# A decoder block's input projection: the last 40 tiles as 2 x 2 blocks with seven half-depth products

## The reference

```python
h = rms_norm(x, norm_g)
proj = h @ w_in            # 1024 -> 8704 columns
u_ssm, z_ssm, q, k, v, z_attn, q_mem, z_mem, gate_logits = split(proj)
y = gelu(s5_ssm(u_ssm)); y = y * sigmoid(y @ w_glu + b_glu); o_ssm = y * silu(z_ssm)
o_attn = dilated_window_attention(q, k, v)  # 3 groups of 4 heads, dilation 1, 4, 16
o_attn = (o_attn weighed by softmax of the groups' log sums) * silu(z_attn)
o_mem = cross_attention(q_mem, rms_norm(mem) @ w_mem_kv) * silu(z_mem)
gates = sigmoid(gate_logits + b_gate)
merged = sum over branches of gates * (o_branch @ w_branch)
out = rms_norm(x + merged @ w_out)
```

## Time and profile before

| | before |
|---|---|
| median of three runs | 2456.7 us |
| span of the profiled execution | 2455.0 us |
| TensorE busy | 2438.3 us (99%), 12622 matmuls |
| DVE busy | 1397.7 us (57%) |
| ACT busy | 588.0 us (24%) |
| GpSimd busy | 190.4 us (8%) |
| mean granted TensorE clock | 0.999 |

### The profile page before, as it was taken

One profiled execution on the slowest core, in us unless ns is written; L12 is line 12 of the kernel. 1 busy time (PEld: TensorE's weight loads), 2 busy tenths in 40 slices (PEclk: granted clock), 3 DMA queues, 4 the chain that ended last, 5 costly groups with the idle time before them and its releaser, 6 DMA issues.

```text
span 2455.0 us, 31834 instructions
## 1 busy us (share of the span) xinstructions
PE 2438.3 (99%) x12622; PEld 1981.9 (81%) x12622; DVE 1397.7 (57%) x2636; ACT 588.0 (24%) x1275; POOL 190.4 (8%) x328
## 2 busy tenths in 40 slices
PE   9999999999999999999999999999999999999998
PEld 8888888888877777787777788888888888888887
DVE  7356776767734444413544443444345778787785
ACT  5222222222211111113333343333251111110201
POOL 0000000000011111110000000011100000000000
PEclk9999999999999999999999999999999999999999
DMA  8232433343454444442332343477654865857571
GB/s 327 99 93 76 106 114 117 107 120 95 115 151 137 149 160 142 151 156 73 105 134 95 121 147 122 161 228 243 205 206 164 285 182 168 248 177 242 159 233 59
DMA packets 171033, 378.67 MB, mean 154 GB/s; under 512 B 27008, under 2 KB 72164, under 8 KB 163717
## 3 DMA queue, kind: packets, MB, share of 16 engines
q1 hardware_dynamic: 134980, 235.03, 31.0%
q0 software_dynamic: 34864, 139.51, 16.9%
q10 hardware_dynamic: 1040, 2.10, 0.2%
HBM read 245.10 MB, written 131.43 MB: 153 GB/s over the span
## 4 chain that ended last, share of the span: by engine, by line
PE 97%; DVE 1%; ACT 1%; issue 0%; DMA 0%; DVEq 0%; SPq 0%; ACTq 0%
PE bank L137 29%; PE bank L139 29%; PE bank L138 28%; PE bank L2285 2%; PE bank L2328 1%; PE bank L2306 1%; PE bank L2194 1%; PE bank L2197 1%; PE bank L2264 1%; PE bank L2180 1%; PE bank L2242 1%; PE bank L2316 1%; ACT tsc L1188 1%; PE bank L2145 0%; PE bank L2247 0%
## 5 line engine op out<-in xcount | busy, mean ns | idle before, releaser
L137 PE MATMUL bank<-h_hi,w_hi 128*128 128x512 f32 (+1 forms) x2720 | 1083.7, 398 | 1.4 <-DVE h_lo L1434 1.4
L139 PE MATMUL bank<-h_hi,w_lo 128*128 128x512 f32 (+1 forms) x2720 | 1057.4, 389 | 0.0
L138 PE MATMUL bank<-h_lo,w_hi 128*128 128x512 f32 (+1 forms) x2720 | 1056.3, 388 | 0.0
L137 PEld LDWEIGHTS bank<-h_hi,w_hi 128*128 128x128 f32 x2720 | 510.8, 188 | 117.2 <-issue 13.6
L139 PEld LDWEIGHTS bank<-h_hi,w_lo 128*128 128x128 f32 x2720 | 510.7, 188 | 108.1
L138 PEld LDWEIGHTS bank<-h_lo,w_hi 128*128 128x128 f32 x2720 | 511.3, 188 | 103.0 <-issue 1.7
L129 DVE CAST w_hi<-w_raw 128x1024 fp32r<-128x1024 f32 (+1 forms) x121 | 83.3, 688 | 310.1 <-PE bank L139 294.3
L137 PE MATMUL bank<-h_hi 128*128 128x512 f32 (+1 forms) x464 | 172.5, 372 | 2.7 <-issue 1.5
L139 PE MATMUL bank<-h_hi,h_lo 128*128 128x512 f32 (+1 forms) x464 | 170.4, 367 | 0.0
L138 PE MATMUL bank<-h_lo,h_hi 128*128 128x512 f32 (+1 forms) x464 | 170.3, 367 | 0.0
L956 POOL DMA_DIRECT2D proj_d<-ev x160 | 88.9, 556 | 931.5 <-ACT ev L1148 560.1
(11 more groups left out here) (267 smaller groups left out, 2166.6 us busy)
## 6 DMA issues: line engine op xcount, KB each, us to landing
proj_d<-ev POOLq DMA_DIRECT2D x160, 256.0 KB, 2.9
w_raw<-w_in SPq DMA_DIRECT2D x68, 512.0 KB, 4.9
gt<-proj_d POOLq DMA_DIRECT2D x32, 768.0 KB, 7.6
proj_d<-ev POOLq DMA_DIRECT2D x22, 1024.0 KB, 4.9
w_raw<-w_br SPq DMA_DIRECT2D x32, 512.0 KB, 4.2
wx_raw<-w_br SPq DMA_DIRECT2D x32, 512.0 KB, 4.5
o_d<-ev POOLq DMA_DIRECT2D x12, 1024.0 KB, 6.9
ev<-o_d SPq DMA_DIRECT2D x12, 768.0 KB, 4.4
```

Of the source, the lines that this page charges most:

```text
L137: nc.tensor.matmul(out, ah, bh, start=(start and n == 0), stop=False)
L138: nc.tensor.matmul(out, ah, bl, start=False, stop=False)
L139: last = nc.tensor.matmul(out, al, bh, start=False, stop=(stop and n == len(pairs) - 1))
```

## The change

The last 40 tiles are no longer done unit by unit. They are cut into 40 blocks, each of two tiles by two token chunks: blocks 0 to 7 are the z tiles on chunks 2 and 3, blocks 8 to 27 all twenty tile pairs on chunks 0 and 1, blocks 28 to 39 the gate tiles on chunks 2 and 3. The depth of 1024 is the third axis, halved in two times four steps. Of such a 2 x 2 x 2 product Strassen's scheme makes seven products of half depth where the plain one makes eight; each factor is a sum or difference of two quarters (or one quarter), and the results are sums and differences of the products.

The work of a block:

- **Token operands.** The seven operands are sums of quarters of h. GpSimd forms them in tiles 6 to 20 (`make_operands`, 72 sums of 128x512) and stores them in DRAM (`hx_d`). They are loaded into the places of h as these come free, rounded by ACT and subtracted by DVE, in two halves of 128x1024 each (`operand_hi`, `operand_lo`). This happens at the start (five of seven) and at two swaps, during blocks 7 and 8 and during blocks 27 and 28 (all seven).
- **Weight factors.** One DMA of 1 MB per block, in place of 512 KB per tile; every weight is loaded twice. GpSimd makes five sums of 128x512 in two buffers (`sum_factor`), ACT rounds all seven factors (`factor_hi`), DVE subtracts (`factor_lo`). The cast and the subtraction of the whole tile on DVE are gone.
- **Products.** Four steps of three matmuls each, in three banks: 0, 1 and 2 start a bank, 3, 4 and 5 add to what is in it, 6 starts again (`product_ready` has the waits).
- **Results.** ACT copies four banks out raw (`keep_raw`), DVE makes three sums with a bank (`bank_sum`), GpSimd three sums of buffers (`outer_sum`), then ACT applies SiLU or tanh in place (`finish_part`) and GpSimd's queue stores four pieces (`store_part`).
- **Side work.** The slots keep their content and their number, eight per block, but come every three and a half steps, after steps 3, 7, 10, 14, 17, 21, 24 and 28 of a block's 28.

The core of the diff:

```diff
+        NPR, NBK, NPAIRS = 7, NT - N_Z, (NT - N_Z) // 2
...
+        O_SLOT = ((0, 0), (0, 1), (2, 1), (1, 1), (3, 0), (2, 0), (3, 1))
...
+        OPERAND_AT = (3, 4, 5, 7, 8, 9, 11)
+        SWAPS = (N_SILU - 1, N_SILU + NPAIRS - 1)
...
+        def triples_before(j):
+            return 7 * (j + 1) // 2
...
+        def product_bank(b, i):
+            return psum[(b + (0, 1, 2, 0, 1, 2, 0)[i]) % 3]
```

On GpSimd:

```diff
+                def sum_factor(b, i):
...
+                    nc.gpsimd.tensor_tensor(w_sum[q % 2][:, :, :], a_half(a, k), a_half(c, m),
+                                            op).then_inc(ws_done[0], 1)
...
+                def after_product(b, i):
...
+                    if i == 0 and b:
+                        store_part(b - 1, 3)
+                    if i == 2:
+                        outer_sum(b, 0)
+                    if i == 4:
+                        outer_sum(b, 1)
+                    if i == 5:
+                        outer_sum(b, 2)
+                        store_part(b, 0)
+                    if i in (1, 2, 3, 4, 6) and b + 1 < NBK:
+                        sum_factor(b + 1, {1: 0, 2: 2, 3: 3, 4: 4, 6: 6}[i])
+                    if i == 6:
+                        store_part(b, 1)
+                        store_part(b, 2)
```

On ACT:

```diff
+                def after_product(b, i):
...
+                    if i == 1:
+                        keep_raw(b, 1)
+                        keep_raw(b, 0)
+                    if i == 4:
+                        keep_raw(b, 4)
+                        finish_part(b, 0)
+                    if i == 5:
+                        keep_raw(b, 5)
+                    if i == 6:
+                        for part in (1, 2, 3):
+                            finish_part(b, part)
+                    if i >= 2 and b + 1 < NBK:
+                        for w in {2: (0, 1), 3: (2, 3), 4: (4,), 5: (5,), 6: (6,)}[i]:
+                            factor_hi(b + 1, w)
```

On DVE:

```diff
+                def bank_sum(b, part):
+
+                    s1, s4 = ring[:, BUF_C22, :], ring[:, BUF_C11, :]
+                    if part == 0:
+                        dve.wait_ge(*count(mul_done, NPR * b + 3))
+                        dve.wait_ge(*count(raw_out, 4 * b + 1))
+                        ins = nc.vector.tensor_tensor(s4, s4, product_bank(b, 2)[:, :], ALU.subtract)
+                    elif part == 1:
+                        dve.wait_ge(*count(mul_done, NPR * b + 4))
+                        dve.wait_ge(*count(sum_out, 3 * b + 1))
+                        dve.wait_ge(*count(pool_sum, 3 * b + 1))
+                        ins = nc.vector.tensor_tensor(s4, product_bank(b, 3)[:, :], s4, ALU.add)
...
+                def after_product(b, i):
...
+                    if i in (2, 3, 6):
+                        bank_sum(b, (i - 2) % 3 if i < 6 else 2)
+                    if i == 0 and 0 < b < NBK:
+                        factor_lo(b, 6)
+                    if i >= 3 and b + 1 < NBK:
+                        for w in {3: (0, 1), 4: (2, 3), 5: (4,), 6: (5,)}[i]:
+                            factor_lo(b + 1, w)
```

On TensorE:

```diff
-                            project(n, c, half)
...
+                for b in range(NBK):
+                    for i in range(NPR):
+                        g = NPR * b + i
+                        product_ready(b, i)
+                        a_hi, a_lo = factor(i)
+                        b_hi, b_lo = operand(h_hi, i), operand(h_lo, i)
+                        for k in range(4):
+                            mm = three_pass(product_bank(b, i)[:, :],
+                                            [((a_hi[:, k, :], a_lo[:, k, :]), (b_hi[:, k, :], b_lo[:, k, :]))],
+                                            start=(k == 0 and i in (0, 1, 2, 6)), stop=(k == 3),
+                                            onto=(3 <= i <= 5))
+                            if k == 3:
+                                mm.then_inc(mul_done[0], 1)
+                            for j in slots_in(g):
+                                if triples_before(j) == 4 * g + k + 1:
+                                    side_slot(j)
```

More of the change, by code:

```diff
@@ L1840, in _ @@
+                for n in range(1, N_Z):
                     done = units_through(n - 1)
-                    split_pair(dve, NKV + (n + 1) // 2, lambda s: (mm_done, done), KD if n + 1 < NT else KS,
-                               slots=((n + 1) % 2,))
+                    if n + 1 < N_Z:
+                        split_pair(dve, NKV + (n + 1) // 2, lambda s: (mm_done, done), KD, slots=((n + 1) % 2,))
                     if n == N_TAB:
```

499 lines of the change are left out of this document (386 added, 113 removed).

## The result

The changed kernel takes 2682.2 us (median of four runs, 2674.74 to 2686.25) where the one before takes 2456.3 (four runs, one more than in the table of before): 1.092 times as long, 95% interval 1.0899 to 1.0936. The forecast was 2396, faster. It was wrong in sign and by 286 us.

A forecast was written before the change was run, and what follows sets the result against it. The kernel was taken as bound by the number of matmul columns on TensorE. 2455.0 - 108.9 + 27.6 (attention) + 13 (swaps) + 8 (rest) = 2394.7 us, with the runs' median 2396; forecast 2370 to 2425, range 2345 to 2442.

The forecast's parts named there:

- What goes: Last 40 tiles, TensorE: 3840 matmuls become 3360; the 480 removed at 0.2268 us take off 108.9 us.
- I take 0.69 ... no bound: GpSimd's block sums: 0.69 us each from DVE's row of the same operation, 10 us of 24.4, so no bound.
- GpSimd's sums hold up DVE: Rival, SSM stage: GpSimd sums and two-SBUF-input DVE instructions exclude each other; +42, 2438 us; chance 0.18.
- Stores at no cost: Transfers in the changed stages, operand sums written and weights read twice among them: cost 0.
- The operand sums at 0, covered by DVE's idle quarter: 72 sums under tiles 6 to 20: cost 0, since even 50 us of table delays would fit DVE's idle time.
- Attention: Attention legs: two beats are 7 steps instead of 8, and work stands ahead on DVE and ACT; 27.6 us, bounds 4.6 and 51.
- the last group: Attention legs with eight exponentials of 128, already late before; four lose the missing three matmuls whole: 2.7 us.
- the forecast's list: Attention legs' waits: 0.24 us per two-beat leg, plus delays from slots 2, 3 and 4 of 2.05, 3.43 and 1.3 us.
- Swaps: Operand swaps at blocks 7 to 8 and 27 to 28: DVE falls behind; 13 us together, bounds 0 and 30.
- Clock: Rival: TensorE's clock falls in the new waits; +17 for 50 us of waits, 2413 us; chance 0.07.

The follow-up runs named there:

- E15: E12 with the places of its longest single waits mended, such as operand sums at the idle end of table units; nothing left out: 2416.4 us.
- E1: Changed kernel with the eight GpSimd sums of a block on 32 columns instead of 512, factors rounded from unsummed data: 2529.7 us.
- E10: E6 with block sums (except block 0's factor sums) and operand sums on DVE, attention minima ahead of copies: 2516.5 us.
- E12: E10 with DVE and ACT work placed where inputs become ready, operand sums over tiles 2 to 7, some loads exchanged: 2456.3 us.
- E13: E12 with extra GpSimd adds that no instruction waits for, 22 of 128x96 per block in blocks 2 to 39: 2496.5 us.
- E2: Changed kernel with each block's fourth piece stored from a constant tile, so the next raw copy waits for no store: 2624.9 us.
- E3: Changed kernel without the 72 GpSimd operand sums under tiles 6 to 20, plain depth tiles stored instead: 2648.5 us.
- E4: Changed kernel with the edits of E1, E2 and E3 together: 2462.7 us.
- E5: E4 with DVE's first side slot at products 3 to 5 ahead of product work, ACT's slots after steps 24 and 28 behind it: 2467.8 us.
- E14: E12 without the two operand swaps (loads, roundings and subtractions left out): 2440.6 us.
- E6: Changed kernel, nothing left out, with GpSimd's outer sum 0 and fourth-piece store earlier and ACT finishing part 1 behind product 5: 2619.6 us.

## Why the prediction was wrong

- **What goes: right.** 12142 matmuls; E15 has TensorE busy for 2350.7 us, near the 2329.4 of the sum, and the rest is clock.
- **"I take 0.69 ... no bound" for GpSimd's sums: the step that failed.** The size was wrong by two (1.40 us, with 3.35 as my upper end), and so was the form. I compared loads, 10 us of 24.4; at 1.40 they would be 11.2 + 4.5, still no bound, and indeed GpSimd is 47% busy. What counted is that a sum stands in one queue with the stores and behind a wait for the 1 MB load, that other queues wait for it, and that DVE stands still beside it. E1 puts all of this at 153 us; E10, with the sums on DVE, shows it from the other side.
- **The rival "GpSimd's sums hold up DVE" had a true mechanism, not the size.** The exclusion is real: by line the 512-column subtractions take 752 to 1394 ns in the mean, and 685 to 697 in E12, which has no such sums after block 0. The forecast's 2438 for it priced only DVE's throughput. The Trainium skill ("SBUF — State Buffer", "Who interferes with whom") says that a DVE instruction with two SBUF inputs contends with a GpSimd instruction that reads SBUF, and that the one that comes later is blocked; the trace agrees on the blocking, with single subtractions of 1.65 to 2.21 us for 0.68, though by its records the cast of 5.84 us had started 0.25 us ahead of the adds that held it. The estimate of 1.12 us a sum from the Trainium skill ("GPSIMD Engine Reference", section 3.1) is below the 1.40 measured. DVE lost 100.8 us of busy time to the blocks' sums (E1). In E13 39.7 us of such loss, from 400 us of short adds, cost the kernel up to 40 us.
- **Stores at no cost: wrong.** The ring through C22 had no term at all. E2: 57 us, of which the clock is a part. The number to compute was the way round (bank sum, function, queue, 5.4 us of landing) against the two products until the copy.
- **The operand sums at 0, covered by DVE's idle quarter: wrong.** E3: 34 us. TensorE waits for tables whose chain runs through DVE without a gap, and adds in a row of four stop DVE for up to 5 us at once (the three casts of 5.8 us). The forecast had allowed 50 us of delay on DVE; it was 76.9, and it did not fall into DVE's idle time. An average of 76.8 in 100 said nothing about that; E15 put the sums, on DVE, at the end of each table unit, and there they cost nothing.
- **Attention: right, 27.6 us.** E4, with GpSimd's sums cut short, has 36.4: outside the last group 20.6 against my 24.9, wait by wait near the forecast's list, and 15.8 against 2.7 in the last group, which was the mis-sized part. In the changed kernel 57.3. The list does not say what another order would give: E5 took the bank sums from ahead of the copies, and its turns waited 42.7 us.
- **Swaps: right**, 13 against 15.7 in E14. That is in E12's order; in the changed kernel products wait 22.7 us for new operands, 5.8 of them at block 0.
- **Clock: a rival at +17, really +110.** The price per us of wait was near: 3.3 for 9.5 (0.35) in the earlier trace rows, 110.5 for 227.9 (0.48) here, 31.4 for 81.0 in E4 and 21.3 for 48.4 in E15 (0.39 and 0.44). There were 227.9 us of new waits where I had given it 50; and it belongs in every forecast with waits, not in a rival.

What stays open: how E1's 153 us divide between late sums and slowed DVE instructions in the changed kernel itself, and why the 256 KB stores land in 5.4 us there and in 3.6 in E12. GpSimd's adds alone don't do it: in E13, with 400 us of them, it is 3.4, and in E1, with its sums cut to 32 columns, still 5.2. In E6, where only the order in two queues differs, it is 4.2.
